# Decode stage of a two-layer attention and convolution block: when page fetches and value gathers are begun, and how the layer norm's mean is summed

## The reference, cut to what matters

```python
mu = jnp.mean(xf, -1, keepdims=True)                      # layer_norm of the convolution
var = jnp.mean(jnp.square(xf - mu), -1, keepdims=True)
...
kc_full = jnp.concatenate([gather_pages(cache_k_cmp[l], page_table), kc], 1)   # also vc_full
ks_full = jnp.concatenate([gather_pages(cache_k_slc[l], page_table), ksl], 1)
vs_full = jnp.concatenate([gather_pages(cache_v_slc[l], page_table), vsl], 1)
kcmp = rms_norm(compress_rows(kc_full, ...), kc_norm[l])   # a small MLP over blocks of rows
_, sel = lax.top_k(imp, n_sel)                             # blocks chosen by the compressed scores
o = gates[..., 0:1] * o_c + gates[..., 1:2] * o_s + gates[..., 2:3] * o_w
```

## Time and profile before

| | us |
|---|---|
| median of 3 runs | 1859.29 |
| lowest, highest | 1858.38, 1865.89 |
| the profiled execution's own time | 1857.72 |
| its span | 1855.9 |
| PE (matmul) busy | 1814.2, 98% |
| DVE (VectorE) busy | 1236.1, 67% |
| ACT (ScalarE) busy | 379.9, 20% |
| POOL (GpSimd) busy | 118.5, 6% |
| mean DMA rate | 108 GB/s |

### The profile page before, as it was taken

How to read it: one execution, slowest core, us unless ns; L and a number is a source line. 1 busy time by engine, 2 the same in 40 slices (tenths; PEclk the granted TensorE clock), 3 DMA queues, 4 the chain that set the end, 5 groups by cost and what they waited for, 6 DMA issues and landing times.

```text
span 1855.9 us, 28046 instructions
## 1 busy us (share of the span) xinstructions
PE 1814.2 (98%) x10726; PEld 1406.8 (76%) x10726; DVE 1236.1 (67%) x2736; ACT 379.9 (20%) x993; POOL 118.5 (6%) x218
## 2 busy tenths in 40 slices
PE   8999999989999999999999999998999999999999
PEld 7767767877777777777777676787877777777777
DVE  5899797652676676673268997966526676676631
ACT  2013376332100001100001134853321100000000
POOL 1011400100000000000000114001000000000000
PEclk9999999999999999999999999999999999999999
DMA  7302564853112122131242045058331212123111
GB/s 278 130 1 82 148 215 144 259 192 138 49 68 91 69 74 86 59 137 63 81 156 76 1 118 149 2 184 284 128 123 47 90 69 91 69 76 111 65 63 51
DMA packets 110536, 200.15 MB, mean 108 GB/s; under 512 B 13409, under 2 KB 81266, under 8 KB 105410
## 3 DMA queue, kind: packets, MB, share of 16 engines
q1 hardware_dynamic: 91090, 162.13, 25.8%
q0 software_dynamic: 5488, 29.93, 4.6%
q10 hardware_dynamic: 13824, 6.30, 1.3%
HBM read 190.62 MB, written 15.94 MB: 111 GB/s over the span
## 4 chain that ended last, share of the span: by engine, by line
PE 92%; DVE 4%; issue 2%; ACT 1%; DMA 1%; SPq 0%; ACTq 0%; DVEq 0%
PE ps L1102 31%; PE ps L1167 15%; PE ps L626 8%; PE ps L661 8%; PE ps L613 7%; PE ps L765 5%; PE ps L958 4%; PE ps L832 2%; PE ps L869 2%; PE ps L851 2%; PE ps L1036 2%; PE ps L903 1%; PE ps L669 1%; PE ps L705 1%; PE ps L918 1%
## 5 line engine op out<-in xcount | busy, mean ns | idle before, releaser
L2229 DVE TENSOR_TENSOR xT<-xT,ps 128x288 f32<-128x288 f32 (+3 forms) x55 | 41.7, 758 | 153.2 <-PE ps L1167 153.0
L1102 PE MATMUL ps<-catT,rD 128*128 128x288 f32 x528 | 131.6, 406 | 0.0
L1547 ACT ACTIVATE rD<-rD 128x592 f32<-128x592 f32 x44 | 30.7, 697 | 450.2 <-DVE rD L2171 450.2
L1102 PEld LDWEIGHTS ps<-catT,rD 128*128 128x128 f32 x528 | 100.3, 190 | 27.7
L1102 PE MATMUL ps<-catT,XC 128*128 128x288 f32 x480 | 119.8, 406 | 0.4 <-DVE rD L2143 0.4
L1102 PE MATMUL ps<-rA,WR 128*128 128x288 f32 x448 | 117.8, 406 | 0.0
L1102 PEld LDWEIGHTS ps<-catT,XC 128*128 128x128 f32 x480 | 91.0, 190 | 26.2 <-issue 1.2
L1268 ACT ACTIVATE rC<-ps 128x256 f32<-128x256 f32 (+8 forms) x162 | 57.5, 386 | 249.8 <-PE ps L661 118.9
L1102 PEld LDWEIGHTS ps<-rA,WR 128*128 128x128 f32 x448 | 85.1, 190 | 23.5
L626 PE MATMUL ps<-catT,WR 128*128 128x288 f32 x384 | 98.8, 410 | 2.0 <-ACT catT L1268 1.1
L613 PE MATMUL ps<-rA,WR 128*128 128x288 f32 x384 | 93.4, 406 | 0.0
(11 more groups left out here) (402 smaller groups left out, 3523.2 us busy)
## 6 DMA issues: line engine op xcount, KB each, us to landing
WR<-in_w_up SPq DMA_DIRECT2D x56, 512.0 KB, 3.7
WR<-in_kvc SPq DMA_DIRECT2D x128, 128.0 KB, 2.3
rB<-in_w_up SPq DMA_DIRECT2D x32, 512.0 KB, 4.4
rD<-in_kvc SPq DMA_DIRECT2D x96, 128.0 KB, 2.3
rD<-in_w_down SPq DMA_DIRECT2D x8, 1408.0 KB, 7.6
rB<-in_ksT SPq DMA_DIRECT2D x160, 64.0 KB, 3.3
rB<-in_w_down SPq DMA_DIRECT2D x6, 1408.0 KB, 8.0
WR<-in_w_glu SPq DMA_DIRECT2D x16, 512.0 KB, 3.6
```

Source lines behind the costliest of these rows:

```text
L1102: ins = mm(ps[:, bank, 0:HN], w[:, k, :], h[:, k, :], start=k == 0, stop=k == 3)
L2229: step(tt(x, x, src, ALU.add))
```

## The change

Five edits. None changes the computed result but by the order of the sum in the mean.

1. `gather_values(l, p + 1)` waits for `imp_kept` of pass p + 1 too, when p is 0 or 1: the gathers are issued in the pass that uses them. Those of passes 0 and 3 stay.
2. SP fetches the window and new values of pass 2 in pass 1, behind the keys of pass 2, and no longer at the end of pass 0 ahead of them. Those of pass 3 stay.
3. ScalarE's 16 key transfers stand in four groups, 4, 6, 3 and 3. The last 3 stand behind the first `keys_kept`, ahead of `keys_squared`.
4. VectorE adds the four channel tiles with three additions of 128x576 (`channel_sums`, behind the second `gelu_in` of the prompt), and `means` multiplies that one sum with ones: two products in the program in place of eight.
5. In `compress` the one step of `hidden` stands ahead of `keys_T(NCP)`, no longer behind it.

The helper `pages` moves to the outer level, and `fetch_cmp` and `fetch_keys` take a range of pages whose default is all 16.

```diff
@@ gpsimd, layer
                     if p + 1 < NPR:
+                        if p + 2 < NPR:
+                            pool.wait_ge(sh["imp_kept"], NPR * l + p + 2)
                         gather_values(l, p + 1)
@@ sync, layer
                     elif p == 1:
                         fetch_keys(l, 2, (0,))
+                        fetch_window(l, 2)
+                        fetch_new(l, 2)
                         sp.wait_ge(*count("hid_made", 2))
                         fetch_cmp(l, 6)
                     sp.wait_ge(*count("pv_done"))
-                    if p + 2 < NPR:
-                        fetch_window(l, p + 2)
-                        fetch_new(l, p + 2)
+                    if p == 1:
+                        fetch_window(l, 3)
+                        fetch_new(l, 3)
@@ tensor, means
-                for c in range(CT):
-                    pe.wait_ge(*count("conv_made"))
-                    for hf in range(2):
-                        ins = mm(ps[:, 2 + hf, 0:HN], ones[:, :], catT[:, CT + c, hf * HN:(hf + 1) * HN], start=c == 0, stop=c == CT - 1)
+                pe.wait_ge(*count("mu_in"))
+                for hf in range(2):
+                    ins = mm(ps[:, 2 + hf, 0:HN], ones[:, :], lnsq[0][:, hf * HN:(hf + 1) * HN], start=True, stop=True)
                 ins.then_inc(sh["mu_made"], 1)
@@ tensor, compress
                 prompt_values()
+                hidden(l, 2, 3, 0, js=range(14, 15))
                 keys_T(NCP)
-                hidden(l, 2, 3, 0, js=range(14, 15))
@@ scalar, decode
                     if more:
-                        fetch_keys(range(7))
+                        fetch_keys(range(4))
...
                         thirds_kept(0)
-                        fetch_keys(range(7, 13))
+                        fetch_keys(range(4, 10))
...
                         tanhed(tanh[1 if p < 2 else 2], NCS)
+                        fetch_keys(range(10, 13))
+                        keys_kept(NCS, KcT[ba % 4])
                         fetch_keys(range(13, 16))
-                        keys_kept(NCS, KcT[ba % 4])
                         keys_squared(NCS)
@@ vector
+            def channel_sums():
+                step(tt(lnsq[0], catT[:, CT, :], catT[:, CT + 1, :], ALU.add))
+                step(tt(lnsq[0], lnsq[0], catT[:, CT + 2, :], ALU.add))
+                tt(lnsq[0], lnsq[0], catT[:, CT + 3, :], ALU.add).then_inc(sh["mu_in"], 1)
...
                 gelu_in(1, NCM, 0, 7)
+                channel_sums()
                 key_means(NCP)
```

More of the change, by code:

```diff
@@ L313, in thirds, with pages @@
             return [ps[:, bank, P * i:P * (i + 1)].rearrange("p (m h) -> p m h", h=2) for i in range(3)]
+        def pages(b, engine):
+            return nc.values_load_multi_w_load_instructions(pgs[0:1, b * 16:(b + 1) * 16], engines=[engine], min_val=0, max_val=NPOOL - 1,
+                                                            skip_runtime_bounds_check_because="page_table holds indices of pages of the pool")[1]
         def rows_at(b):
@@ L349, in qkv, with fetch_cmp @@
                 sp.dma_start(WD[:, ch % 2, 0:KD * CHW], I["w_qkv"][l, ch]).then_inc(sh[f"wd_in{ch % 2}"], 16)
[L351 to L358, removed]
+            def fetch_cmp(l, b, gs=range(16)):
+                at, page = rows_at(b), pages(b, mybir.EngineType.SP)
+                for g in gs:
                     sp.dma_start(kvc[at][:, 256 * g:256 * (g + 1)],
-                                 I["kvc"][l, ds(page, 1)].rearrange("a p e -> (a p) e")).then_inc(sh[f"kv_in{at}"], 16)
+                                 I["kvc"][l, ds(page[g], 1)].rearrange("a p e -> (a p) e")).then_inc(sh[f"kv_in{at}"], 16)
             def fetch_window(l, p):
@@ L370, in fetch_new, with fetch_keys @@
                 sp.dma_start(vn[:, :, P:2 * P], O["s_v_win"][l, two, WIN - DS:WIN].rearrange("e s h d -> s e (h d)")).then_inc(sh[f"new_in{p % 2}"], 16)
-            def fetch_keys(l, p, es=(0, 1)):
+            def fetch_keys(l, p, es=(0, 1), gs=range(16)):
                 for e in es:
-                    for g, page in enumerate(pages(2 * p + e)):
+                    page = pages(2 * p + e, mybir.EngineType.SP)
+                    for g in gs:
                         sp.dma_start(ksT[e][:, P * g:P * (g + 1)],
-                                     I["ksT"][l, ds(page, 1)].rearrange("a p e -> (a p) e")).then_inc(sh["ks_in"], 16)
+                                     I["ksT"][l, ds(page[g], 1)].rearrange("a p e -> (a p) e")).then_inc(sh["ks_in"], 16)
             def down(l, m, a=0, b=FT):
@@ L1448, in decode @@
                         act.wait_ge(sh["pages_in"], 16)
-                        pages = nc.values_load_multi_w_load_instructions(pgs[0:1, (2 * p + 3) * 16:(2 * p + 4) * 16],
-                                                                         engines=[mybir.EngineType.Activation], min_val=0, max_val=NPOOL - 1,
-                                                                         skip_runtime_bounds_check_because="page_table holds indices of pages of the pool")[1]
+                        page = pages(2 * p + 3, mybir.EngineType.Activation)
                     def thirds_kept(i):
@@ L1463, in fetch_keys @@
                             act.dma_start(ksT[1][:, P * g:P * (g + 1)],
-                                          I["ksT"][l, ds(pages[g], 1)].rearrange("a p e -> (a p) e")).then_inc(sh["ks_in"], 16)
+                                          I["ksT"][l, ds(page[g], 1)].rearrange("a p e -> (a p) e")).then_inc(sh["ks_in"], 16)
                     act.wait_ge(*count("cmp_max"))
```

2 lines of the change are left out of this document (1 added, 1 removed).

## The result

The changed kernel takes 1850.06 us (median of 5 runs, 1848.30 to 1854.27), the kernel before 1859.29 beside it: a ratio of 0.995, with a 95% interval of 0.9933 to 0.9967. It is 9.2 us faster, where 19.1 were forecast, and the time lies 0.06 us above the range of 1834 to 1850. Run again 12 times it took 1851.23 beside 1861.27, ratio 0.9951 (0.9936 to 0.9965).

What follows compares the result with a forecast made beforehand. TensorE, busy for 98% of the span, was taken to bound the kernel. 10.5 + 4.9 - 1.0 + 3.5 - 2.7 + 3.9 = 19.1 us off 1857.7 gives 1838.6, with the median 1.6 above it 1840.2; range 1834 to 1850.

Steps and rivals of the forecast that it cites:

- The stall: First product of `third(1, 0)` in pass 2, both layers: TensorE's waits for sequence 6's rows go, 10.5 us won.
- The half clock behind it: TensorE's 5.8 and 4.0 us at half clock after the pass 2 waits go, 4.9 us won.
- B: Pass 2: sequence 6's rows are late for another reason, so 15.4 us stay and the time is 1856; chance 0.06.
- rival A: Pass 1: the wait moves to sequence 7's rows or late values, costing 4 to 10 us, 1844 to 1850; chance 0.12.
- Rival C: Passes 1 and 2: gather gets an equal turn among three queues, values land late, slower at 1862; chance 0.04.
- or the clock falls elsewhere: Sign that the prediction is wrong: the granted clock drops at other places than the pass 2 waits; no size given.
- What the gathers meet in pass 2: Moved gathers run beside other transfers; keys and window are needed a pass later, and in pass 2 two more thirds hide it.
- The exponential: Pass 1: ScalarE's six issues ahead of it are slowed beside the moved gather, 0.5 us a layer, 1.0 us lost.
- `PcT`: Pass 1, ScalarE's copy: with three issues fewer ahead and no gather beside, its wait goes, 3.5 us won, bounds 2.5 and 3.5.
- `keys_squared`: Three issues ahead delay it 0.45 us in passes 0, 1, 2 of both layers, 2.7 us lost, bounds 0 and 4.
- the sum of edit 3: ScalarE's key groups 4, 6, 3, 3: 3.5 us won at `PcT` less 2.7 lost at `keys_squared`.
- The mean: `compress`: four records instead of sixteen and the moved step start `keys_T(NCP)` 1.95 us earlier a layer, 3.9 us won.

Runs made afterwards that it cites:

- slab 0 ahead: Changed kernel, but in pass 2 SP fetches slab 0 of `w_out` behind six of its sixteen key transfers: 1845.13 us, 0.9940; run again 1851.16, 0.9953.
- slab 0 ahead with 5, 5, 6: Changed kernel with slab 0 of `w_out` behind six of SP's keys and ScalarE's key transfers in groups of 5, 5, 6: 1847.28 us, 0.9954.
- 5, 5, 6: Changed kernel with ScalarE's key transfers in groups of 5, 5 and 6, the six ahead of `keys_kept`: 1853.71 us, 0.9975.
- 6, 5, 5: Changed kernel with slab 0 of `w_out` behind six of SP's keys and ScalarE's key transfers in groups of 6, 5, 5: 1843.60 us, 0.9917.

## Why the prediction was wrong in size

9.9 us are missing. The largest part is edit 3, put at 0.8 won and measured at 3.7 to 5.9 lost; the half clock gave about 2.7 less than its 4.9, and slab 0, put at nothing, waited 2.4. These overlap, since the clock is in the time of edit 3 too.

**The stall, 10.5 us: right.** 9.6 are gone (0.9 left); one edit, edit 1, does it. What is left of it in the fourteen profiles with edit 1 is 0 in eight and up to 2.6 us in the others (the first of slab 0 ahead). Rivals B and C are out: rows and values wait little, the gathers of pass 1 landed 6.3 and 8.1 us after issue, and no wait for them stands in the changed kernel's list. Of rival A one part came true, in layer 1 of the kernel with edit 1 alone, 0.9 us for the values, and 0.2 to 2.0 us in three others (edit 2 undone, with and without slab 0 ahead, and slab 0 ahead with 5, 5, 6). Rival C's equal turns can be seen where three queues are busy, 34.9, 34.7 and 34.5% in the microsecond shown above; but from 347 to 356 us, while the gather of pass 1 runs, it has 61.6%, since the other two are not busy throughout.

**The half clock behind it, 4.9 us: right for edit 1 alone, not for the whole.** Alone it brought 4.6. With all edits the mean clock over 12 runs was 0.9953 against 0.9941 beside it: 0.0012 x 1861 = 2.2 us. By the spread of the runs that difference is uncertain by about 2.6 us either way, and the five first runs of the changed kernel have 0.9968 (that of before beside them is not on record), so the loss against 4.9 is likely but not sure. Two stretches take it. One is the 10.2 us behind the mean, in five of the fourteen profiles with edits 4 and 5, 5.1 us lost each time. The other is the new stretch at 365 us. It came in the six profiles in which TensorE stood idle in L1040 for 1.13 to 1.63 us late in pass 1 of layer 0 (the changed kernel twice, edit 2 undone, 5, 5, 6, 6, 5, 5 and the second of slab 0 ahead) and in none of the eleven other profiles, the kernel before among them, where that idle time was 0 to 0.92 us. The length of a gap does not decide it alone: in layer 1 half clock followed gaps of 0.82 and 0.96 us in L1040's place, and did not follow 1.28 (L1038) and 1.74 us (L628) in the kernel with edit 1 alone or 1.52 us (L631) in the changed kernel's second profile. The prediction named "or the clock falls elsewhere" as a sign of being wrong, and gave it no price.

**What the gathers meet in pass 2, put at nothing: a step that failed.** The prediction followed SP's keys and window beside the gather of pass 1, "needed a pass later", and left out the next thing in SP's queue, slab 0 of `w_out`, wanted 9.1 and 6.5 us behind its issue in the two layers: 2.4 us here, 1.5 in the second profile, 2.8 in edit 1 alone. These are waits; that a kernel without them is faster is not shown (slab 0 ahead). The exponential, forecast at 1.0, cost 1.2 and 1.7 in the changed kernel (1.8 and 2.3 against 0.6) and 2.0 in edit 1 alone. Edit 1 was put at 14.4 us and measures 6.9.

**`PcT`, 3.5: right. `keys_squared`, 2.7: nearly right** as a wait (1.7 and 2.0 in the two profiles, 2.4 alone), though its cause was larger: 4.9 us of delay over six passes and not 2.7, since an issue beside heavy traffic took up to 1.42 us and not 0.4. **The step that failed most is the sum of edit 3**, 0.8 won: it loses 3.7 alone and 4.5 to 5.9 beside the others. The term that it put at nothing is the transfers themselves ("a risk of a few tenths, kept in the range"): they land later and push others, 3.2 us of waits alone; in the changed kernel 1.5 for keys in the second profile and none in the first. What else it loses beside the others is open. It may be the clock: the idle time of L1040, after which the stretch at 365 us came, is 0.21 us with edit 3 undone and 1.35 and 1.31 with it, but no kernel here moved that idle time alone.

**Edit 2, 0: right. The mean, 3.9: right in size** (3.9 measured alone, 1.5 to 6.5), with 0.31 us of wait at `gelu_out` where 0.4 were forecast, but in part by luck. The 1.95 a layer compares the two starts of `keys_T(NCP)`, although the step of `hidden` stands ahead of it in one kernel and behind it in the other; by the prediction's own rows the gain is 3.1 - 0.4 = 2.7. Against that stands the wait of `keys_second`, which it did not see. The first product behind all of this starts at 206.28 in place of 207.95, 1.7 us a layer.

One sum on record does not come out of its terms: with 1.0 for the mean, 4 for `keys_squared` and 3.8 for the exponential the forecast's worst is 10.5 + 4.9 + 3.5 - 3.8 - 4 + 1.0 = 12.1, or 1847; it is 1850 only with `PcT` at 2.5 and 2.0 us of late values besides.

Edits alone give 6.9 + 3.9 - 3.7 = 7.1 us; all together gave 9.2, each with an interval of about 2.4 us to either side.

## What to carry to other kernels

When a transfer is moved out of the way of one need, list everything that each queue still has to deliver in its new time, with the moment of need, down to the first weights of the next stage; the stall goes, and the next item in the queue takes its place. Splitting an engine's issues moves the bytes too, so price them on the DMA engines beside the issue time, and give each group no more issues than the engine has idle time at that place. When two instructions change places, compare the start of the first one behind both. A microsecond of idle TensorE is worth more than itself when a stretch at half clock follows it: read the granted clock in several executions before putting a price on one.

## What the runs showed of the hardware

**Instruction packets stop TensorE and hold up the issuing engines.** The view of transfers lists packets of kind instruction on queue q8, 16 KB each, 85 of them in either kernel: pieces of the program on their way to an engine. From 361 to 362.3 us in the changed kernel:

```profile
q1 hardware_dynamic: 214, 0.24, 59.5%
q10 hardware_dynamic: 367, 0.17, 46.8%
q8 instruction: 1, 0.02, 5.3%
issues: line engine op xcount, KB each, median us to landing
rD<-in_kvc SPq DMA_DIRECT2D x2, 128.0 KB, 3.9
```

That packet is on its way from 361.10 to 362.20. L1040 stops at 362.35 and goes on at 363.70, 1.50 us behind the packet's end. In all twelve profiles with such a gap there, from 0.21 to 1.63 us long, products went on 1.31 to 1.50 us behind the end of a 16 KB packet. A count settles what they wait for. In the seventeen profiles L1040 (or its like, such as L1036 of before) stands idle 23 times with "issue" as the releaser; counting TensorE's instructions from 1 (products, weight loads and semaphore instructions in the order in which they start), it goes on with number 5058, 15,042, 15,810 or 17,602 each time, a weight load, and these lie multiples of 256 apart. So TensorE waits for the next 256 of its own instructions. Issues of ScalarE and SP in flight beside such a packet are long as well: 1.42 us from 361.15 and 1.12 us from 361.47, both over at 362.6, and 1.66 us in the kernel before, from 363.87 beside the packet of 363.90 to 365.15. All three end 0.37 to 0.38 us behind the packet. The Trainium skill, "Runtime: NRT & Kernel Launch", section "Instruction fetch mechanics", has an engine's instructions refilled in blocks of 16 KiB while the current one runs, and calls the cost of crossing a block "mostly hidden". The block size agrees with the rows; hidden it was not in twelve profiles at this place. By that page's 256 instructions a block, 85 packets are 21,760, near TensorE's 10,702 products and as many weight loads, which makes the queue TensorE's.

The prediction had no term for these gaps, and edit 4 moves them: it takes 24 instructions a layer out of the stream, so the same numbers fall on other products. Number 17,602 falls on L1036 in pass 3 of layer 1 in the three kernels without edit 4, with gaps of 0.64, 1.28 and 1.01 us; with edit 4 it falls on L631 or its like, without a gap. The row of the kernel before:

```profile
1352.91 0.30 PE L1036 MATMUL ps<-rA,rC 8*32 8x64 f32 x5 [0.64 <-issue]
```

Number 5058 falls into L1036 or its like with and without edit 4, and there the gap came only in kernels that hold edits 1 and 4. Why the packet is late for them stays open: in the changed kernel it begins at 361.10, in the one before at 358.12, and no kernel here moved it alone.

**The clock varies from run to run** of the same kernel. The 12 runs of the changed kernel have means from 0.992 to 0.999 and times from 1861.35 to 1846.26 us, in nearly the same order; so 0.007 of mean clock is worth some 14 us. Most of the spread of these measurements is that.
